# Attention of a decoder trunk in split float32: the order of value products, exponentials and gate turns in the first two pairs of query tiles

## The reference, cut to what matters

```python
def block(args):                       # one tile of 128 queries
    s = (einsum('bqhd,bkhd->bhqk', qn, k_nope) + einsum('bqhr,bkr->bhqk', qp, k_pe)) * scale
    s = where(causal, s, -inf)
    p = softmax(s, axis=-1)
    return einsum('bhqk,bkhd->bqhd', p, v)
...
o_mla = mla_attention(...) * silu(g_mla)
```

## Time and profile before

| | us |
|---|---|
| median of 3 runs (lowest, highest) | 938.72 (937.49, 941.99) |
| the profiled execution, its own time | 938.28 |
| its span | 936.6 |
| PE busy | 856.3 (91%) |
| DVE, ACT, POOL busy | 596.9, 381.6, 258.1 |
| turns 0 to 31 of the attention | 200.0 to 300.4 |
| turns 32 to 63 | 300.4 to about 430 |

### The profile page before, as it was taken

The page is one execution under the profiler, slowest core; times in us unless marked ns, Lnnn a source line. Parts: engine busy times, 40 slices in busy tenths (PEclk is TensorE's granted clock), DMA queues, the critical chain, the costliest instruction groups (busy, mean ns, idle before and its releaser), DMA issues.

```text
span 936.6 us, 12171 instructions
## 1 busy us (share of the span) xinstructions
PE 856.3 (91%) x4136; PEld 679.3 (73%) x4136; DVE 596.9 (64%) x983; ACT 381.6 (41%) x731; POOL 258.1 (28%) x259
## 2 busy tenths in 40 slices
PE   7999999987777989998899899999899999999995
PEld 6898775755445666667787588888678888888884
DVE  6988789455444676773687154368996676654453
ACT  6253325654344555661323265325433546221120
POOL 2000002612020182000696633001955013142243
PEclk9999999996798999998999999999999999999998
DMA  9011265000000030003422311033733223012111
GB/s 330 23 28 41 70 86 119 24 3 1 1 1 1 1 113 1 1 1 116 132 90 91 112 45 46 1 112 102 213 113 123 79 68 136 23 65 71 46 45 67
DMA packets 40685, 64.19 MB, mean 69 GB/s; under 512 B 8256, under 2 KB 21824, under 8 KB 40608
## 3 DMA queue, kind: packets, MB, share of 16 engines
q1 hardware_dynamic: 40624, 63.42, 22.4%
HBM read 52.33 MB, written 9.44 MB: 66 GB/s over the span
## 4 chain that ended last, share of the span: by engine, by line
PE 58%; DVE 22%; ACT 7%; issue 7%; DMA 3%; POOL 1%; SPq 1%; DVEq 0%; ACTq 0%; POOLq 0%
PE psum L1941 32%; PE psum L2255 15%; PE psum L1950 4%; PE psum L2028 4%; DVE probT_lo L1753 2%; DVE negmax L1678 2%; PE psum L2168 2%; DMA ln_gb<-ln_b_dram 1%; PE psum L1976 1%; ACT probT_hi L1286 1%; ACT prob L1247 1%; DVE vg_lo L1813 1%; DMA wgs_raw<-even_w_in_dram 1%; DMA xT_raw<-x_cols_dram 1%; DVE x_lo_raw L1845 1%
## 5 line engine op out<-in xcount | busy, mean ns | idle before, releaser
L1753 DVE TENSOR_TENSOR probT_lo<-psum,probT_hi 128x512 fp32r<-128x512 f32 (+2 forms) x96 | 53.5, 558 | 63.1 <-ACT probT_hi L1286 60.8
L2255 PE MATMUL psum<-vg_hi,x1T_hi 128*128 128x512 f32 x208 | 82.1, 395 | 5.5 <-DVE vg_lo L1813 5.5
L2255 PE MATMUL psum<-vg_lo,x1T_hi 128*128 128x512 f32 x208 | 81.7, 393 | 0.0
L2255 PE MATMUL psum<-vg_hi,x1T_lo 128*128 128x512 f32 x208 | 81.6, 392 | 0.0
L2028 PE MATMUL psum<-kT,qTt 96*128 96x512 f32 (+2 forms) x192 | 79.8, 529 | 0.1
L1286 ACT ACTIVATE probT_hi<-psum 128x512 fp32r<-128x512 f32 (+2 forms) x96 | 47.1, 490 | 63.1 <-PE psum L1950 59.8
L1678 DVE TENSOR_REDUCE negmax<-psum 128x1 f32<-128x128 f32 (+3 forms) x64 | 48.5, 758 | 22.5 <-PE psum L2032 21.2
L1247 ACT ACTIVATE prob<-psum,negmax 128x128 f32<-128x128 f32 (+3 forms) x64 | 47.4, 740 | 32.5 <-issue 25.9
L2168 PE MATMUL psum<-probT_hi,V 128*128 128x256 f32 (+1 forms) x160 | 44.2, 307 | 14.2 <-DVE gate L1723 9.7
L1950 PE MATMUL psum<-ident,prob 128*128 128x128 f32 x288 | 48.5, 299 | 9.4 <-DVE probT_lo L1753 5.3
L1065 POOL TENSOR_TENSOR zn<-zn,ln_gb 128x512 f32<-128x512 f32 x16 | 23.1, 1443 | 106.9 <-DMA ln_gb<-ln_b_dram 92.6
(11 more groups left out here) (404 smaller groups left out, 2201.3 us busy)
## 6 DMA issues: line engine op xcount, KB each, us to landing
vg_piece<-odd_w_in_dram SPq DMA_DIRECT2D x60, 256.0 KB, 3.2
x_res<-x_dram SPq DMA_DIRECT2D x8, 512.0 KB, 4.2
wqk_raw<-odd_w_in_dram SPq DMA_DIRECT2D x8, 512.0 KB, 5.1
x_scratch<-zn SPq DMA_DIRECT2D x8, 512.0 KB, 2.9
w_out_raw<-odd_w_out_dram SPq DMA_DIRECT2D x4, 1024.0 KB, 5.0
V<-x_scratch SPq DMA_DIRECT2D x8, 512.0 KB, 4.6
out_dram<-SG SPq DMA_DIRECT2D x8, 512.0 KB, 2.9
xT_raw<-x_cols_dram SPq DMA_DIRECT2D x7, 512.0 KB, 8.6
```

The source lines that it names most:

```text
L1753: step.frees(vec.tensor_tensor(lo, source, hi.bitcast(F32), ALU.subtract), ("pt", number))
L2255: mm = pe.matmul(bank(*job), lhsT, rhs, start=(k == 0 and j == 0 and product not in ADDS_TO), stop=(k == 3 and j == len(pairs) - 1), skip_ ...
```

## The change

Five edits, all in the order of steps. The number and kind of instructions of each engine stays as it was.

1. `values_turn`: in turns 5, 9, ... 29 both value products of two heads stand together at the turn's start (before: `av` 2j in turn 4j+3, `av` 2j+1 in turn 4j+5). `av` 14 and 15 stand together in turn 32.
2. ACT computes `exponentials(n + 3)` behind the copies of turn n while n+3 is a short turn.
3. In `attention_steps`, `gT` and `ob` are last in their turn, behind `q` and `s`, in all 64 turns; `output_parts` stands behind the copies of `pt`.
4. DVE, short half: `gate_scaled` moves from the start of turn 4j+6 to the end of the `pt` step of turn 4j+5, and `output_gated` from the start to the end of that step in turn 4j+7.
5. `q` and `qT` sit in other turns: `q` in r = 0, 1, 3, 4 for p = 0 (before 0 to 3) and 3, 4, 5, 7 later (before 3, 5, 6, 7); `qT` in r = 9, 11 (before 10, 11) and 0, 1 (before 1, 2), where r = n mod 16.

```diff
         def values_turn(n):
-            return n > 2 and n % 2 == int(n in SHORT)
+            if n == len(SHORT) or n % 4 == 1 and n in SHORT:
+                return ((n - 4) // 4 * 2, (n - 4) // 4 * 2 + 1)
+            if n % 2 == 0 and n - 2 not in SHORT:
+                return (n - 2) // 2,
+            return ()
...
                 yield "pt", n
-                if n in OUTPUT_TURNS:
-                    yield "gT", OUTPUT_TURNS.index(n)
-                    yield "ob", OUTPUT_TURNS.index(n)
-                if p and r in (1, 2):
-                    yield "qT", (2 * p + r - 1, 1)
-                if p < 3 and r in (10, 11):
-                    yield "qT", (2 * p + r - 8, 0)
...
+                if p and r in (0, 1):
+                    yield "qT", (2 * p + r, 1)
+                if p < 3 and r in (9, 11):
+                    yield "qT", (2 * p + 2 + (r == 11), 0)
+                for key in queries_at(p, r):
+                    yield "q", key
                 if n + 4 in SHORT:
                     yield "s", n + 4
                 if n + 2 < len(heads) and n + 2 not in SHORT:
                     yield "s", n + 2
+                if n in OUTPUT_TURNS:
+                    yield "gT", OUTPUT_TURNS.index(n)
+                    yield "ob", OUTPUT_TURNS.index(n)
...
# ScalarE, step "pt"
-                    if n % 2 == 0 and n >= 4:
+                    if n % 2 == 0 and n + 1 not in SHORT:
                         exponentials(n + 1)
-                    if n in OUTPUT_TURNS:
-                        output_parts(OUTPUT_TURNS.index(n))
...
-                    if n % 2 and 4 <= n + 1 < len(heads):
+                    if 4 <= n + 3 and n + 3 in SHORT:
+                        exponentials(n + 3)
+                    if n % 2 and n + 1 < len(heads) and n + 1 not in SHORT:
                         exponentials(n + 1)
+                    if n in OUTPUT_TURNS:
+                        output_parts(OUTPUT_TURNS.index(n))
...
# VectorE, step "pt"
-                    if n in OUTPUT_TURNS:
+                    if n in OUTPUT_TURNS and n not in SHORT:
                         gate_scaled(OUTPUT_TURNS.index(n))
-                    if n - 1 in OUTPUT_TURNS:
+                    if n - 1 in OUTPUT_TURNS and n - 1 not in SHORT:
                         output_gated(OUTPUT_TURNS.index(n - 1))
...
+                    if n + 1 in OUTPUT_TURNS and n + 1 in SHORT:
+                        gate_scaled(OUTPUT_TURNS.index(n + 1))
+                    if n - 1 in OUTPUT_TURNS and n - 1 in SHORT:
+                        output_gated(OUTPUT_TURNS.index(n - 1))
```

More of the change, by code:

```diff
@@ L489, in scores, with queries_at @@
             return psum[:, b0:b0 + len(score_banks(n)), :].rearrange("p a b -> p (a b)")[:, 0:w], b0 * 512
-        OUTPUT_TURNS = [4 * j + (6 if 4 * j + 5 in SHORT else 4) for j in range(STEPS // 2 - 1)]
+        OUTPUT_TURNS = [4 * j + (6 if 4 * j + 6 in SHORT else 4) for j in range(STEPS // 2 - 1)]
         def values_turn(n):
-            return n > 2 and n % 2 == int(n in SHORT)
+            if n == len(SHORT) or n % 4 == 1 and n in SHORT:
[3 more added lines that the diff above has]
+            return ()
+        def queries_at(p, r):
+            places = (3, 4, 5, 7) if p else (0, 1, 3, 4)
+            if p < 3 and r in places:
+                return (2 * p + 2 + places.index(r) // 2, places.index(r) % 2),
+            return ()
         def attention_steps():
@@ L500, in attention_steps @@
                 p, r = divmod(n, 16)
-                if values_turn(n):
-                    yield "av", (n - 2) // 2
+                for m in values_turn(n):
+                    if m >= 0:
+                        yield "av", m
                 yield "pt", n
-                if n in OUTPUT_TURNS:
-                    yield "gT", OUTPUT_TURNS.index(n)
-                    yield "ob", OUTPUT_TURNS.index(n)
-                if p and r in (1, 2):
-                    yield "qT", (2 * p + r - 1, 1)
-                if p < 3 and r in (10, 11):
-                    yield "qT", (2 * p + r - 8, 0)
-                if p < 3 and r in ((3, 5, 6, 7) if p else (0, 1, 2, 3)):
-                    nth = ((3, 5, 6, 7) if p else (0, 1, 2, 3)).index(r)
-                    yield "q", (2 * p + 2 + nth // 2, nth % 2)
+                if p and r in (0, 1):
[4 more added lines that the diff above has]
+                    yield "q", key
                 if n + 4 in SHORT:
```

## The result

The kernel before ran in 938.42 us (median; 937.49 to 941.99), the changed one in 915.54 us (914.42 to 919.38). The ratio is 0.9757, 95% interval 0.9718 to 0.9795.

The account below looks back on a forecast made before the run. PE, busy 91% of the span, was taken as the bound, losing time to waits and a low clock. Short half 10.3, long half 2.0 and clock 0 sum to 12.3 us off: 926.4 us median, range 916 to 935.

Parts of the forecast that it names:

- the clock's term: Turns 0 to 31: low clock costs 13 us and falls stay about as many; term 0, bounds -13 to +4.5.
- the new wait: PE at ob waits for o_parts behind ACT's exponentials: 2.1 to 2.7 us per full group, about 12 us in sum.
- The order in the short half: Turns 0 to 32 at equal clock: reordering takes off 10.3 us, bounds 5 to 15.
- the walk: Chain timing of four-turn groups across PE, ACT and DVE; a second-pair group without q or qT goes from 11.5 to 10.4 us.
- The long half: From turn 32: scores cover the o_parts waits, each of eight groups ends 0.25 us earlier; 2.0 us off, bounds -1 to 4.
- the clash: Long half: POOL subtraction slows a DVE gate product to 2.43 us, PE waits 2.4; scores would cover 1.3; priced at 0.
- The clock stays up: Rival, short half: less PE idle returns most or all of the 13 us; 913 to 918 us; chance 0.14.
- A larger new wait: Rival: ACT or DVE reaches turn 4j+9's maximum later, each 0.7 us costing 5 in seven groups; 931 to 935; chance 0.18.
- a low clock throughout: Rival, short half: long ob waits hold the clock at 1.2 GHz; 943 us (941 to 947); chance 0.06.
- the lead's wait: Exponentials three turns ahead delay o_parts, so ob waits about 12 us in sum; the lead removes 3.8 us of prob waits.

Follow-up runs that it names:

- p4: Kernel before with only the change's new places of q and qT; long half 128.1 us.
- v: Kernel before with only the value products of two heads put together in the first two pairs; short half 80.7 us, profiled execution 921.7 us.
- p1: Kernel before with only the exponentials of the first two pairs three turns ahead instead of one; gives 1.6 us, ratio not distinguishable from 1.
- e4: Kernel after with output_parts put ahead of the exponentials of turn n+3 on ACT; short half 72.8 us.
- p3: Kernel before with only gate turn and output product behind the scores on PE; 9.9 us gained in the short half, long half 122.6 us.
- e8: Kernel after with output_parts ahead of the exponentials in turns 6 to 30 and DVE's gate products ahead of the low half in the short half; 904.6 us.
- e3: Kernel after with the old order of gate turn, output product and output_parts from turn 32 on; 924.5 us, long half 128.1 us.
- m1: Kernel after with the exponentials one turn ahead, as before; short half 69.7 us, kernel 3.9% under the kernel before.
- e1: Kernel before with 4 idle matmuls before the gated-output wait and 6 before the value product's bank claim, first two pairs; 0.3% slower, clock 1.00.
- e6: Kernel before with 2 idle matmuls before the gated-output wait and 3 before the value product's bank claim; 926.4 us, short half 89.5 us.
- e5: Kernel after with 3 idle matmuls before the gated-output wait in each of the first seven groups; short half 78.4 us.
- e2: Kernel after with 6 idle matmuls before the gated-output wait in each of the first seven groups; 914.5 us, short half 82.7 us.
- e7: Kernel after with output_parts ahead of the exponentials in turns 6 to 30 alone; 905.4 us, long half 120.6 us.
- e9: e8 with 2 idle matmuls before the gate's wait in the first three groups; gets back 2.3 us in turns 9 to 13, beats both kernels.

## Why the prediction was wrong

**The step that failed: the clock's term, put at 0.** The text had the right evidence (13 us lost to a mean of 0.81) and argued that the falls would come in much the same number, as the new wait is longer than any before, so that the 13 us stay. Measured: the low clock cost 11.3 us before and 3.7 after, so the term was -7.6. The number of falls was nearly right, five before and four after; the step from it to the cost was not, since the time at the lower level went from 37 to 13 us, and PE's work in it from 30.6 to 13.3. At the text's own price of 0.44 per us of work that is an estimate of 13.6 and 5.9 us, 7.7 apart. Turns 21 to 32 kept the upper level from end to end, with output waits of 1.1 and 1.7 us in them. The waits of PE between turn 5 and turn 32, added up from the timeline (those of 0.2 us and more; number, sum), beside the clock of the half:

```
before  22   22.6 us   0.81      after   14   15.3 us   0.92
p4      18   21.4 us   0.80      v       19   13.3 us   0.94
p1      20   24.9 us   0.85      e4      14   10.3 us   0.98
p3      16   18.4 us   0.87      e8      11    8.4 us   0.95
e3      15   14.8 us   0.92      m1      13    7.4 us   1.00
```

The clock goes with the sum, with p1 and e8 a little out of line. Each line is one execution. The text looked at the longest wait where it should have looked at all the idle; it named the sum (18 against 28 us) only in favour of a rival, at 0.14. That the clock moves with the sum is shown over these kernels; that idle is the cause is shown by e1 and e6, which changed nothing else but PE's idle. Why a fall ends sooner in the kernel after stays open.

**The order in the short half: right.** 10.3 forecast (bounds 5 to 15); with the idle filled on both sides, 89.5 against 78.4 us, 11.1 (some 12 if e5's turns 5 to 9, at 0.84, are put at e2's time). By groups, forecast and then e6 less e5: turns 0 to 5 0 and -0.4, 5 to 13 1.0 and 0.6, 13 to 17 1.2 and 1.4, 17 to 25 4.0 and 4.9, 25 to 29 1.4 and 1.2, 29 to 32 2.7 and 3.4. Turns 17 to 25 were to take 24.2 us and take 24.1 in e5 (28.2 and 29.0 in the order of before). Here the walk was good to about 1 us for a group or two of them where the clock is known.

**The new wait: right in place, over-priced.** 2.1 to 2.7 us per group forecast, 1.1 to 1.8 measured. The walk let PE reach `ob` without the gate turn's own wait (0.64 us in the rows above), which comes ahead of it and is taken off it. The end of the group hardly moved by that.

**The long half: 4.2 for 2.0.** The groups without the clash sum to 2.2, the size foreseen, but by luck: the text had it from the gate turn behind the scores, 0.25 in each of eight groups, and p3, which has that place alone, gives 0.5 in these seven groups, as PE waits for the low half instead of `o_parts`. The other 1.7 came only with the new places of `q` and `qT` on top, which the text did not price there (alone they cost 3.4). The rest of the 4.2, 2.0 us, is the group of turns 44 to 48 (16.1 to 14.1 us), where the clash had cost a wait of 2.4 us and a fall of the clock behind it (350.7 to 354.1 us). The text knew that the scores would cover 1.3 of it, and took 0 because the clash might double. It came again, once, and was covered, in p3 too (a gate product of 2.44 us, group at 14.5). In e6, in the order of before, it was missed by a shift of the start, and the group took 14.2.

**The rivals.** "The clock stays up" came nearest: it said 913 to 918, and 915.5 lies in it. Its mechanism was half right: the mean rose, not to 1.00 but to 0.92, and gave 7.6 us and not 13; order (0.8) and long half (2.2) made up part of the rest. A larger new wait and a low clock throughout both failed. The Trainium skill, "TensorE: Matmul & The Clock Gate", section "A second HAM failure mode: psum-queue depth-cycling", was read as speaking against a gain from merging waits. The measurement says the reverse: fewer waits, 14 instead of 22, single ones as long as before (up to 1.8 us against 1.9), gave a higher clock. Its main statement, that repeated short idles cost clock, holds in e6: filling them alone gave 0.81 to 1.00.

**What was not foreseen at all:** that one of the parts costs more than it brings. The text priced the lead's wait at 12 us and its gain at 3.8, and went on to price the whole; leaving it out was in those two numbers.

## What to carry to other kernels

When a stage shows PE partly idle and its granted clock under 1, price two things: the idle on the path, and the busy time that comes back when idle shrinks; here the second was two thirds of the first. Matmuls that nobody reads, put into the waits and shorter than they are, separate the two, with one run of each kernel. And price the parts of a composite change one by one: a wait that the own forecast adds with one part is a reason to try the change without that part.

## What the runs showed of the hardware

- The clock fell behind idle stretches of PE and stayed up when they were filled: 0.81 to 1.00 in e6, with outputs and order untouched. But the sum alone does not fix it: e8 idles less than e7 in the half (8.4 us against 9.1) and has the lower clock (0.95 against 0.98), its fall coming behind a single wait of 2.0 us for `qTt`. In e9 a wait of 1.96 us at the same place was followed by none (1.00 from 210 to 230 us). In the kernel after, a wait of 1.7 us was followed by a fall at 244 us and by none in turns 25 to 29. Which pattern of idle it takes stays open.
- Executions of one kernel differ in the clock and with it in time: for the kernel before, the shortest of 45 took 933.2 us at 0.977, the longest 944.7 at 0.961, and as a rule the higher clock goes with the shorter time.
- At the lower level (1.2 GHz) `q` takes twice the time, transposes and value matmuls less. From the start of a piece to that of the next work a `q` takes 2.56 against 1.29 us, four transposes 0.81 against 0.46, eight value matmuls 1.74 against 0.97. From first start to last end it is 2.76 against 1.46 for the `q` and 1.02 against 0.62 for the transposes.
- A DVE product of two SBUF inputs that begins behind the start of a POOL subtraction of 2.34 us ends 0.3 us after it: begun 0.2 us behind it is 2.43 us long, 0.57 behind 2.05, 1.19 behind 1.45 (e3), where it takes 0.43 alone. Which order of work meets the clash is settled by shifts of a few us: e6 missed it, p3 and m1 met it (2.44 and 2.10 us).
